# Latents skewed by one tile, attention's row maxima spread, and a long convolution with early loads, its bias in the filter and 512-wide sums

## The reference

```
def centred_long_conv(z, h):                 # L tokens, through a transform of length n
    y = irfft(rfft(z, n=2L) * rfft(h, n=2L), n=2L)
    return y[:, L // 2: L // 2 + L]

def hyena_mixer(u, short_w, short_b, filt, bias):
    v, x1, x2 = split(depthwise_conv(u, short_w, short_b), 3)
    h = hyena_filters(L, *filt)
    z = v
    for n, gate in enumerate((x1, x2)):
        z = gate * (centred_long_conv(z, h[n]) + bias[n] * z)
    return z

q = (rmsnorm(u_q, q_norm_g) @ w_uq)          # 8 heads of 64 + 32 columns, each part rms-normalised, rotated
kv = (rmsnorm(c_kv, kv_norm_g) @ w_ukv)      # 8 heads of 64 (keys) + 64 (values)
p = softmax((q_nope k_nope' + q_rope k_rope') * MLA_SCALE);  out = p v
```

## Time and profile before

| | us |
|---|---|
| three runs | 3706.1, 3712.3, 3716.2 (median 3712.3) |
| the profiled execution, its own time | 3705.0 |
| its span | 3703.4 |
| PE busy in the span | 3292.6 (89%) |
| DVE busy in the span | 1614.9 (44%) |

### The profile page before, as it was taken

One profiled execution on the slowest core, in us unless ns is written; L12 is line 12 of the kernel. 1 busy time (PEld: TensorE's weight loads), 2 busy tenths in 40 slices (PEclk: granted clock), 3 DMA queues, 4 the chain that ended last, 5 costly groups with the idle time before them and its releaser, 6 DMA issues. The chain is left out here.

```text
span 3703.4 us, 38116 instructions
## 1 busy us (share of the span) xinstructions
PE 3292.6 (89%) x15050; PEld 2528.5 (68%) x15050; DVE 1614.9 (44%) x1944; ACT 945.9 (26%) x1079; POOL 321.7 (9%) x231
## 2 busy tenths in 40 slices
PE   5879987589965588999999999989996999999999
PEld 1338864344535467888888888867775778888887
DVE  5214305646638864222333332357666333333233
ACT  2223112133331022211111111157765231111111
POOL 2000000046640011000000000020000100000000
PEclk8879998779987798999999999989998999999999
DMA  6761210000021131111111111111112211111112
GB/s 251 281 244 64 89 52 0 0 0 1 1 99 76 44 133 34 35 40 35 35 37 38 36 40 35 40 68 34 42 37 80 74 40 46 45 51 45 51 45 74
DMA packets 46018, 228.88 MB, mean 62 GB/s; under 512 B 6776, under 2 KB 7288, under 8 KB 39641
## 3 DMA queue, kind: packets, MB, share of 16 engines
q1 hardware_dynamic: 42456, 205.86, 15.8%
q10 hardware_dynamic: 1728, 13.63, 0.9%
q0 software_dynamic: 1728, 7.87, 0.5%
HBM read 201.65 MB, written 25.69 MB: 61 GB/s over the span
## 5 line engine op out<-in xcount | busy, mean ns | idle before, releaser
L240 PE MATMUL bank<-h_hi,w_hi 128*128 128x512 f32 (+1 forms) x2616 | 705.0, 370 | 13.1 <-DVE h_lo L1563 8.2
L240 PE MATMUL bank<-h_lo,w_hi 128*128 128x512 f32 (+1 forms) x2616 | 704.0, 369 | 8.3 <-issue 8.3
L240 PE MATMUL bank<-h_hi,w_lo 128*128 128x512 f32 (+1 forms) x2616 | 702.7, 369 | 0.0
L226 DVE TENSOR_TENSOR w_lo<-w_raw,w_hi 128x1024 fp32r<-128x1024 f32 x194 | 262.7, 1354 | 674.9 <-ACT w_hi L220 670.5
L240 PEld LDWEIGHTS bank<-h_hi,w_hi 128*128 128x128 f32 x2616 | 453.8, 189 | 100.6 <-issue 15.7
L240 PEld LDWEIGHTS bank<-h_lo,w_hi 128*128 128x128 f32 x2616 | 454.1, 189 | 95.2 <-issue 9.6
L240 PEld LDWEIGHTS bank<-h_hi,w_lo 128*128 128x128 f32 x2616 | 454.1, 189 | 85.8
L1495 DVE SCALAR_TENSOR_TENSOR x<-bank,c_mods,x 128x1024 f32<-128x1024 f32 (+3 forms) x280 | 271.8, 1006 | 256.7 <-PE bank L240 256.6
L220 ACT ACTIVATE w_hi<-w_raw 128x1024 fp32r<-128x1024 f32 x194 | 203.9, 1052 | 648.0 <-PE bank L240 608.8
L240 PE MATMUL bank<-hid_hi,w_hi 128*128 128x512 f32 (+1 forms) x880 | 242.7, 373 | 11.6 <-DVE x L1495 11.6
L240 PE MATMUL bank<-hid_lo,w_hi 128*128 128x512 f32 (+1 forms) x880 | 240.7, 371 | 0.0
(11 more groups left out here) (280 smaller groups left out, 3722.6 us busy)
## 6 DMA issues: line engine op xcount, KB each, us to landing
w_raw<-in_weights SPq DMA_DIRECT2D x194, 512.0 KB, 3.5
ada_w<-in_ada_w SPq DMA_DIRECT2D x32, 1536.0 KB, 7.7
x<-in_x SPq DMA_DIRECT2D x2, 5120.0 KB, 18.7
h_gate<-u_scratch SPq DMA_DIRECT2D x4, 2560.0 KB, 10.1
u_scratch<-uc POOLq DMA_DIRECT2D x12, 640.0 KB, 3.2
spec_lat<-f_spec ACTq DMA_DIRECT2D x2, 3584.0 KB, 10.4
h_spec<-spec_lat SPq DMA_DIRECT2D x2, 3584.0 KB, 17.1
x_kept<-x SPq DMA_DIRECT2D x1, 4096.0 KB, 13.6
```

Of the source, the lines that this page charges most:

```text
L226: e.tensor_tensor(k.w_lo[s][:, :], k.w[s][:, :], k.w_hi[s][:, :].bitcast(F32), ALU.subtract).then_inc(k.split_lo[s], 1)
L240: mm = e.matmul(out[:, c:c + m], w[:, c1:c1 + P], x[:, c:c + m], start=(first and kk == 0 and n == 0), stop=(last and kk == kt - 1 and n = ...
```

## The change

- **prologue and bias.** The bias row is added to the middle tap of each filter (two operations on one partition for each order), so `hyena` no longer adds `bias * z`. The bias row sits where the first weight pair is loaded, so `load_pair` now waits for `xh_ready` 3.
- **even_in.** After the norm has read `x`, GpSimd's queue loads `w_uq`, `w_ukv`, `gq`, `gk` and `cos` (`latent_inputs`), and DVE multiplies the gains in at the block's end (`fold_gains`).
- **latents.** GpSimd's copies go away: PE reads `lat` and `rope` directly. The loop is written out tile by tile with a skew: products of tile t, then the transposes of tile t - 1. Copies out of PSUM have semaphores of their own (`q_out`, `k_out`) and stand in the middle of the next tile's work on ACT and DVE.
- **attention.** `MAX_AT` is every second unit; DVE puts at most one other operation between two maxima; head 0 uses two accumulators for its scores; the constant edge rows are written by ACT; the scaling of head h waits until head h + 2's maxima. SP loads `tf`, the first spectrum, the first gate and `z` for the convolution during heads 6 and 7, for which the tensors are placed anew.
- **hyena.** Only `ti` is loaded at its start. `products` takes four operations instead of six.

```
@@ prologue
             ada.load(k, e)
+            e.wait_ge(xh_ready, 3)
             load_pair(k, e, 0)
...
                 e.wait_ge(hw_ready, (order + 1) * NT)
+                e.wait_ge(bias_landed, 16)
+                for centre, n in ((M_LAT // 2, N_LAT), (M_LAT + M_CTX // 2, N_CTX)):
+                    steps(e.scalar_tensor_tensor(out=hw[0:1, centre, :], in0=bias_row[0:1, order * D_HY:(order + 1) * D_HY],
+                                                 scalar=1.0 / n, in1=hw[0:1, centre, :], op0=ALU.mult, op1=ALU.add), 1)
+                steps.settle()
@@ even_in
+            fold_gains(k, e)
...
         def _(e):
             e.sem_inc(uc_free, 2)
+            e.wait_ge(k.xr_ready, norm.h_base + KT)
+            latent_inputs(k, e)
@@ latents, tensor
+            def products(t):
+                s, cols = t % 2, slice(t * P, (t + 1) * P)
+                if t >= 2:
+                    e.wait_ge(q_out, t - 1)
...
+                if t >= 2:
+                    e.wait_ge(k_out, t - 1)
...
+            e.wait_ge(k.m_folded, 5)
+            products(0)
+            for t in range(1, NT):
+                products(t)
+                turn(t - 1)
+            turn(NT - 1)
@@ latents, scalar
+                e.activation(sqr[:, :], k.bank[:, 4 * s + 1, 384:384 + ROPE], ACT.Square).then_inc(hsq, 1)
+                if t:
+                    queries_out(t - 1)
@@ latents, vector
+                e.tensor_scalar(ss[:, 16:25], ss[:, 16:25], 1.0 / ROPE, EPS, ALU.mult, ALU.add).then_inc(hss, 1)
+                if t:
+                    keys_out(t - 1)
+                e.wait_ge(hsd, t + 1)
@@ attention
-    MAX_AT = [1, 2, 7, 8, 9, 11, 12, 13, 16, 17]
-    SPREAD_AT = [4, 10, 14, 16, 19]
-    SUMS_AT, REFILL_AT = 4, 16
+    MAX_AT = [0, 2, 4, 6, 8, 10, 12, 14, 16, 17]
+    SPREAD_AT = [7, 11, 15, 17, 19]
+    SUMS_AT, REFILL_AT = 5, 16
...
+            e.wait_ge(hi_ready, 2 * HEADS)
+            e.wait_ge(lo_ready, 2 * HEADS)
+            e.dma_start(k.hy_tf[:, :], d["tab_f"]).then_inc(k.hy_landed, 16)
+            e.dma_start(k.hy_spec[:, :, :], d["spec_lat"][0]).then_inc(k.hy_spec_in, 16)
+            e.dma_start(k.hy_gate[:, :, :], hyena_rows(1)).then_inc(k.hy_gate_in, 16)
+            e.wait_ge(slot_full, unit_slot[(HEADS - 1) * UNITS - 1] + 1)
+            e.dma_start(k.hy_z[:, :, :], hyena_rows(0)).then_inc(k.hy_landed, 16)
@@ hyena, products
-                    tt(t[0][:, :], zr, hr, ALU.mult, 1)
-                    tt(t[1][:, :], zi, hi, ALU.mult, 1)
-                    if pos:
-                        e.wait_ge(sp_read, pb[j] + pos)
-                    tt(t[2][:, :], zr, hi, ALU.mult, 1)
-                    tt(t[3][:, :], zi, hr, ALU.mult, 2)
-                    tt(ys[h][:, 2 * pos, :], t[0][:, :], t[1][:, :], ALU.subtract, 1)
-                    e.tensor_tensor(ys[h][:, 2 * pos + 1, :], t[2][:, :], t[3][:, :], ALU.add).then_inc(sp_read, 1)
+                    steps(e.tensor_tensor(real, z2, hr.unsqueeze(1).to_broadcast([P, 2, CH]), ALU.mult), 1)
+                    steps(e.scalar_tensor_tensor(out=t[:, 1, 0, :], in0=z2[:, 1, :], scalar=-1.0, in1=hi, op0=ALU.mult,
+                                                 op1=ALU.mult), 1)
+                    e.tensor_tensor(t[:, 0, 1, :], z2[:, 0, :], hi, ALU.mult).then_inc(sp_read, 1)
                     steps.settle()
+                    e.wait_ge(sp_read, g + 1)
+                    e.tensor_tensor(ys[h][:, 2 * pos:2 * pos + 2, :], t[:, 0], t[:, 1], ALU.add).then_inc(ys_done, 1)
...
-                    for c in range(2):
-                        ct = 2 * h + c
-                        fma(cv[h][:, c, 0:n], z[:, ct, t0:t0 + n],
-                            k.hy_bias[:, order * CT + ct:order * CT + ct + 1], cv[h][:, c, 0:n])
+                    steps.settle()
```

More of the change, by code:

```diff
@@ L1180, in _, with maximum, low_k @@
         def _(e):
-            def low(h):
+            def maximum(h, j):
+                e.wait_ge(s_full, h * NT + j + 1)
+                e.reduce_max(mx[:, h % 2, j:j + 1], score_sums(h, j)[:, 0:T if j < 8 else CTX], AX_X).then_inc(mx_done, 1)
+            def low_k(h):
                 e.wait_ge(hi_ready, 2 * h + 1)
@@ L1187, in low, with invert @@
                                 ).then_inc(lo_ready, 1)
-            def maxima(h, first, end):
-                for j in range(first, end):
-                    e.wait_ge(s_full, h * NT + j + 1)
-                    e.reduce_max(mx[:, h % 2, j:j + 1], k.acc[0][:, 0:T if j < 8 else CTX], AX_X).then_inc(mx_done, 1)
-            def normalise(h):
-                own = slice(64 * (h % 2), 64 * (h % 2) + 64)
+            def invert(h, c):
                 e.wait_ge(slot_read, sum_slot[h] + 1)
-                e.reciprocal(rs[:, :], rs[:, :]).then_inc(ri_ready, 1)
-                e.wait_ge(ri_ready, 2 * h + 1)
+                part = rs[:, c * CTX:(c + 1) * CTX]
+                e.reciprocal(part, part).then_inc(ri_ready, 1)
@@ new lines, in scale_ctx @@
+            def scale_ctx(h):
+                e.wait_ge(ci_ready, h + 1)
+                e.tensor_tensor(attT[64 * (h % 2):64 * (h % 2) + 64, h // 2, LAT:T], ctx_raw[0:64, :], ctx_ri[0:64, :],
+                                ALU.mult).then_inc(ctx_done, 1)
+            maximum(0, 0)
+            maximum(0, 1)
+            low_k(0)
+            maximum(0, 2)
+            maximum(0, 3)
+            low_q(0)
+            for j in range(4, NT):
+                maximum(0, j)
+            for h in range(1, HEADS):
+                maximum(h, 0)
+                low_k(h)
+                maximum(h, 1)
+                low_q(h)
+                maximum(h, 2)
+                if h >= 2:
+                    invert(h - 2, 0)
+                maximum(h, 3)
+                if h >= 2:
+                    invert(h - 2, 1)
+                maximum(h, 4)
+                if h >= 2:
+                    scale(h - 2, 0)
+                    scale(h - 2, 1)
+                maximum(h, 5)
+                if h >= 2:
+                    invert_ctx(h - 2)
+                maximum(h, 6)
+                if h >= 2:
+                    scale_ctx(h - 2)
+                for j in range(7, NT):
+                    maximum(h, j)
```

432 lines of the change are left out of this document (216 added, 216 removed).

## The result

The changed kernel took 3562.1 us, median of four runs (3556.2 to 3566.4), beside 3709.2 us of the kernel before in the same series (3701.7 to 3716.2). The ratio is 0.9603, 95% interval 0.9577 to 0.9628. The forecast was 3593, range 3573 to 3620: the sign is right and the gain was larger than the range allowed. The profiled execution took 3564.4 us.

The account below looks back on a forecast made before the run. Taken as bounds: step order in `latents`, PE in `attention`, DVE in `hyena`. Savings 52.4 + 14.4 + 20 + 1 + 14.9 + 12.6 = 115 us gave 3590 from the profiled execution, 3597 from the median; forecast 3593, range 3573 to 3620.

Parts of the forecast that it names:

- the start: Start of `latents`: with gains folded and tables ready in `even_in`, the first sums come 15.2 us earlier.
- the passes: Tile loop of `latents`: period 12.5 us a tile set by PE's chain; 127.9 us from first sums to end, before 165.1.
- Start of attention: First scores to first unit: edge rows on ACT and two accumulators let DVE's maxima run in a row; 14.4 us saved.
- hyena's start: Start of `hyena`: `z` and `tf` landed during head 7, so PE's wait for loads goes; 14.9 us saved.
- bias: `hyena`: bias operations leave DVE, 10.6 us in latent jobs and 2.0 in context jobs; 12.6 us saved.
- the products: `hyena`: four operations instead of six make a residue 1.99 us where it was 2.00; counted as 0.
- The heads: Heads of `attention`: less waiting for maxima and no lost clock, 38.1 us a head; 20 us saved over seven heads.
- the floor of 36.4: Heads of `attention`: us a head if PE waits for nothing, the upper bound of that gain, 32 us instead of 20.
- That the heads gain nothing: Rival for `attention`: remaining waits still bring the low clock, the 20 us are lost, 3613; chance 0.15.
- slow products in `latents`: Rival for `latents`: PE's short idle in each tile keeps products slow, 18 us less gain, 3611; chance 0.10.
- products that pay by duration: Rival for `hyena`: residues gain by the operations' durations, 11 us more gain, 3582; chance 0.10.
- a VectorE-bound attention: Rival for `attention`: DVE's maxima and other operations set the head, kernel slower, 3705 and above, say 3730; chance 0.02.

Follow-up runs that it names:

- spacing_alone: The kernel before with only the changed kernel's places of the maxima, their transposition and the row sums in attention, VectorE's order old: units 380.2 us, span 3766.7 us.

## Why the prediction was right, and where it failed

- **latents.** Right: the start to 0.1 us, the passes 2 us better. The copy of the queries is what ends TensorE's wait (12.4 us in eight waits of 1.6), as the chain of the prediction says.
- **Start of attention, its tail, hyena's start, bias, the products.** Right: 14.4 and 1.1 in the trace, and by the runs that undo them one at a time 13.7 for 14.9, 13.1 for 12.6 (4 x 2.61 is 10.4, where the prediction has 10.6), and 0 for 0. The wait inside a residue was put at 0.46 us without a row for its 0.04; it is 0.53 (1016.41 to 1016.94). `hyena` as a whole gave 1.7 more than the sum.
- **The heads.** The step that failed is "That leaves 1.7 us of waiting where 2.5 stood. If no clock is lost, a head takes 38.1". The mechanism was right, its size was not: 36.3 us instead of 20. Two figures were wrong. First, I took 3.76 us for the low part as if it belonged to the operation. It belonged to the work that GpSimd then had in a row; in its new place it takes 2.6, so maximum 1 is done when TensorE asks for it, and only 0.3 us of waiting is left in a head. Second, the floor of 36.4 subtracted an average wait (2.5) from the one fast head (38.9). That head had waited 2.9 us, and its products cost more than the wait besides: TensorE was busy for 36.0 us of it, and is for 34.9 of the new head of 35.1. So 1.1 us of busy time went together with 2.7 of idle time, about 0.4 for each of the three waits, and the list of waits doesn't count it. The other 2.1 of the 5.9 us a head (41.0 against 35.1) is the clock, which stays at 1.00. The gain is that of six distances from head to head and not of seven: by the row sums of the two traces (L1195 now) these six came down from 244.7 to 208.9 us, while the row sums of the first head come 52.5 us behind the first unit before and 53.0 after, one unit later in the head than before. The prediction also says that its range leaves out the better bound of the heads. With 32 instead of 20 the forecast is 3581, which lies inside 3573 to 3620: the heads alone (36.3) would not have left the range, it took the next step too.
- **"The feed-forward blocks behind them are not touched, and I leave their time as it is."** This is the second step that failed. It cost 13.7 us, half of the miss. No instruction of the block changed, but its place in the program did, and with it when its loop waits for instructions to be loaded. I had looked for trouble from the longer instruction stream in `latents` only, where none came.
- **The prologue.** Counted at 0. The difference in the profiled pair is +8.7, which is no more than executions of one prologue differ by; a cost of up to 3 us stays open. By luck it hid part of the miss: without it the traces would be 149.3 us apart, where 115 were forecast.
- **Rivals.** That the heads gain nothing, slow products in `latents`, products that pay by duration, and a VectorE-bound attention all fell. But the last shows how near it was: with one half of the edit, units of 332 and 380 us, the case of the other sign came up in both, by the order of the waits and not, as the rival has it, because VectorE was full (it too stood idle up to 8.0 us between maxima of spacing_alone).

## What to carry to other kernels

Before a row's duration is moved to another place, ask what stood beside it there: of two engines that hold each other up, as VectorE and GpSimd here, the length of the one belongs to the schedule of the other. A wait in a chain of short steps costs more than the list of waits says, since restart and clock are paid too; compare busy and idle time of one pass at full clock, not the mean wait. When a program's code grows or shrinks, look at the loops behind it for stops without a releaser and for instruction packets in the DMA view, and try a few idle instructions ahead of them.

## What was unexpected of the hardware

- A loop of TensorE stopped 2.0 to 2.3 us at each of four edges, or not at all, by the number of instructions ahead of it: 1103.5 or 1086.4 us for the same stretch of the same work. The stops are 8.8 us of the 17.1; the clock around them is at 0.91. They go with 16 KB packets of instructions, 81 in the one kernel and 45 in the other.
- A subtraction of 96x1280 with both operands in SBUF took 1.48, 2.6, 3.76 or 6.12 us, by whether none, one, two or four instructions of GpSimd went ahead of it.
- In 9.8 us without work (and 4.1 more ahead of the first scores) the granted clock went to 0.50, TensorE's level of 1.2 GHz, for most of the 35.5 us behind: 0.55 over that window. With transposes without use the like window has 0.87.
